# Third tile's slots written between the two half sums of the next tile, in the routing stage of a two-expert MoE layer

## The reference, cut to what matters

```python
y = mlstm_mixer(h, w_in, b_gates, head_norm_w, w_out)
h = layer_norm(ALPHA * h + y, ln1_g, ln1_b)
# hier_moe(h, ...):
g_top = argmax(h @ w_group + b_group)
within = (h @ w_router + b_router)[the 8 experts of g_top]
top_vals, top_idx = top_k(within, 2)
expert_ids = g_top * 8 + top_idx
# tokens are sorted by expert; each expert works on its own rows
yb = (silu(xb @ w_gate[e]) * (xb @ w_up[e])) @ w_down[e]
h = layer_norm(ALPHA * h + sum of the two weighted yb, ln2_g, ln2_b)
```

## Time and profile before

| | us |
|---|---|
| median of 3 runs | 1147.18 |
| lowest, highest | 1144.99, 1147.30 |
| the profiled execution, its own time | 1145.99 |
| its span in the trace | 1144.1 |
| PE busy | 1117.4 (98%) |
| DVE busy | 788.3 (69%) |
| ACT busy | 625.6 (55%) |

### The profile page before, as it was taken

One profiled execution on the slowest core, in us unless ns is written; L12 is line 12 of the kernel. 1 busy time (PEld: TensorE's weight loads), 2 busy tenths in 40 slices (PEclk: granted clock), 3 DMA queues, 4 the chain that ended last, 5 costly groups with the idle time before them and its releaser, 6 DMA issues.

```text
span 1144.1 us, 15458 instructions
## 1 busy us (share of the span) xinstructions
PE 1117.4 (98%) x5465; PEld 915.0 (80%) x5465; DVE 788.3 (69%) x1104; ACT 625.6 (55%) x692; POOL 209.4 (18%) x183
## 2 busy tenths in 40 slices
PE   8999999999999999999999999999999999999986
PEld 7878889778888787878888888888888888888852
DVE  3310323135455787779999999998988989899646
ACT  4311313213334410037888878788788887888634
POOL 3000111100000000002425312142332332322200
PEclk9999999999999998999999999999999999999998
DMA  7613314401211421138999999999999999999765
GB/s 279 208 50 120 120 45 129 129 19 39 72 39 57 184 93 56 74 152 340 417 389 366 399 378 383 398 383 392 380 374 384 380 391 384 381 397 379 284 272 222
DMA packets 65145, 284.23 MB, mean 248 GB/s; under 512 B 16156, under 2 KB 16156, under 8 KB 39620
## 3 DMA queue, kind: packets, MB, share of 16 engines
q1 hardware_dynamic: 52096, 254.14, 58.2%
q0 software_dynamic: 11840, 25.19, 6.0%
q10 hardware_dynamic: 1156, 4.20, 0.9%
HBM read 266.66 MB, written 33.55 MB: 262 GB/s over the span
## 4 chain that ended last, share of the span: by engine, by line
PE 92%; DVE 3%; DMA 2%; ACT 1%; issue 1%; DVEq 1%; POOL 0%; POOLq 0%; SPq 0%; ACTq 0%
PE bank L1582 26%; PE bank L1584 25%; PE bank L1583 25%; PE bank L1957 2%; PE bank L1846 1%; PE bank L1992 1%; PE bank L1797 1%; PE bank L1799 1%; PE bank L1802 1%; PE bank L1596 1%; PE bank L1755 1%; PE bank L1811 1%; DMA yy<-expert_rows 1%; PE bank L2055 1%; PE bank L1838 1%
## 5 line engine op out<-in xcount | busy, mean ns | idle before, releaser
L1582 PE MATMUL bank<-whi,xghi 128*128 128x512 f32 x512 | 202.5, 396 | 1.0 <-DVE xglo L1436 1.0
L1584 PE MATMUL bank<-whi,xglo 128*128 128x512 f32 x512 | 199.9, 390 | 0.0
L1583 PE MATMUL bank<-wlo,xghi 128*128 128x512 f32 x512 | 199.3, 389 | 0.0
L1424 DVE TENSOR_TENSOR wlo<-raw_down,whi 128x2048 fp32r<-128x2048 f32 x64 | 146.3, 2291 | 27.4 <-ACT whi L792 27.3
L1582 PE MATMUL bank<-whi,xhi 128*128 128x512 f32 x384 | 157.7, 411 | 1.1 <-ACT num L735 0.6
L1583 PE MATMUL bank<-wlo,xhi 128*128 128x512 f32 x384 | 152.6, 397 | 0.0
L1584 PE MATMUL bank<-whi,xlo 128*128 128x512 f32 x384 | 152.2, 396 | 0.0
L1424 DVE TENSOR_TENSOR wlo<-raw,whi 128x2048 fp32r<-128x2048 f32 x64 | 146.3, 2288 | 4.3 <-ACT whi L792 3.4
L1424 DVE TENSOR_TENSOR wlo<-raw_up,whi 128x2048 fp32r<-128x2048 f32 x64 | 146.3, 2285 | 0.0
L792 ACT ACTIVATE whi<-raw_up 128x2048 fp32r<-128x2048 f32 x64 | 122.4, 1914 | 25.8 <-PE bank L1584 25.4
L792 ACT ACTIVATE whi<-raw_down 128x2048 fp32r<-128x2048 f32 x64 | 122.4, 1912 | 23.1 <-PE bank L1584 23.1
(11 more groups left out here) (341 smaller groups left out, 1734.0 us busy)
## 6 DMA issues: line engine op xcount, KB each, us to landing
raw<-l_w_gate SPq DMA_DIRECT2D x64, 1024.0 KB, 8.2
raw_up<-l_w_up SPq DMA_DIRECT2D x64, 1024.0 KB, 8.4
raw_down<-l_w_down SPq DMA_DIRECT2D x64, 1024.0 KB, 8.6
raw<-l_w_in SPq DMA_DIRECT2D x5, 2048.0 KB, 10.2
yy<-expert_rows SPq DMA_DIRECT2D x7, 1024.0 KB, 13.1
xt<-hcat SPq DMA_DIRECT2D x8, 512.0 KB, 4.5
o_rows<-stage POOLq DMA_DIRECT2D x16, 256.0 KB, 2.4
qkT<-qk_rows SPq DMA_DIRECT2D x16, 256.0 KB, 3.9
```

Source lines behind the costliest of these rows:

```text
L1424: tt(wlo[k][:, halves(p)], raw_e[k][:, halves(p)], whi[k][:, halves(p)].bitcast(F32), ALU.subtract).then_inc(e_lo[k], 1)
L1582: t.matmul(out, lh, rh, start=first, stop=False)
L1583: t.matmul(out, lh, rl, start=False, stop=False)
L1584: return t.matmul(out, ll, rh, start=False, stop=last)
```

## The change

`norm_sums(3)` is replaced by its four parts, and `slots(2)` is put between the first and the second of them. No operation is added or taken away, apart from one drain (an instruction that waits until DVE's earlier operations have finished), which `slots` already had in front of it and `half_sums` has too. PE, ACT, POOL and SP have the program of before.

```diff
         residual(3, 0)
         residual(3, 1)
         top_two(2)
-        norm_sums(3)
+        half_sums(3, 0)
         slots(2)
+        half_sums(3, 1)
+        row_sums(3)
+        centre(3)
         norm_rows(3)
```

## The result

| | before | changed |
|---|---|---|
| median, us | 1145.82 (16 runs) | 1149.18 (16 runs) |
| lowest, highest | 1144.75, 1148.71 | 1147.67, 1150.21 |
| span of the profiled execution | 1144.1 | 1147.6 |

The ratio is 1.0022, with a 95% interval of 1.0015 to 1.0028: the change makes the kernel slower by 1.7 to 3.2 us, at the centre 2.5 us. The medians lie 3.36 us apart and the means of the runs 2.76: the times of each kernel fall into groups over a microsecond apart, so the centre depends on how it is taken. The forecast was 1148.3, with +1.1 us; the loss has its sign and is over twice as large. The kernel before was run again beside each set of experiments, with medians of 1147.73 (17 runs), 1147.48 (15) and 1147.31 (31), up to 1.9 us above the 1145.82 here. The changed kernel was not, apart from a single run, so part of the 2.5 us may belong to this set of runs.

The account below looks back on a forecast made before the run. PE, busy for 98% of the span, was taken to bound the kernel. -0.97 us won plus 2.05 us lost at half clock gave +1.08 on the median 1147.18: 1148.26, forecast as 1148.3, range 1145.3 to 1150.2.

Parts of the forecast that it names:

- `slots(2)` ahead lets `token_list(2)` start without a wait: On PE after out_half(4, 0): the wait for r_ohr goes, 2.31 us, with 0.11 us to spare.
- DVE pays nothing: On DVE from 443.40 to 447.31: reordering costs nothing, within 0.16 us either way; norm_rows(3) starts at 447.3 as before.
- PE runs ahead to `ranks(3)` and stands there: PE wins 5.59 us up to ranks(3), then waits 4.62 us for r_a; 0.97 us are left.
- A slow stretch behind `ranks(3)`: PE's dense products behind the wait run at half clock for 4.1 us, costing 2.05 us; bounds 1.7 and 3.4.
- the lower bound of +0.7: Low end of the net loss, +0.7 to +1.4 us, from slow stretches of 3.4 to 4.7 us.
- the low end of the forecast's own range, 1146.1: Own range 1146.1 to 1149.2: net +0.7 to +1.4 on runs 2.2 below to 0.1 above the median.
- The sum of +1.08 us: Whole kernel: -0.97 us won at ranks(3) plus 2.05 us lost at half clock, a loss of 1.08 us.
- It stays to the end: From out_half(4, 1) on: the +1.08 us persists, as PE's wait before ranks(4), 0.23 us at most, absorbs nothing.
- the rival of the later fall: Around 521 us the clock falls, slowing the first expert's products for 3.3 us: +1.65 more, 1149.9 us; chance 0.04.
- The long slow stretch: Rival: the slow stretch behind ranks(3) lasts 6.8 us, +2.4 us, 1149.6 us; chance 0.18.
- the clock hold: Rival behind ranks(3): PE's clock holds; chance 0.10.
- The gain as it looks: Rival at ranks(3): r_a isn't late, or PE keeps its 5.59 us: 1141.6 us; chance 0.06.

Follow-up runs that it names:

- Experiments 3: 18 fillers ahead of ranks(3) in the changed kernel: 1.0013 to before; 9 ahead of token_list(2) and 18 ahead of ranks(3) in the kernel before: 1.0040.
- 6: Changed kernel with inverse(3) and top_two(3) directly behind row_sums(3), and centre(3), shift(3) and residual(4, 0) behind them; ratio to before 0.9972.
- experiment 5: 4 + 4 fillers before and behind the transposes of the first expert's rows, in both kernels; ratios to before 0.9997 (kernel before) and 1.0007 (changed).
- experiment 7: Kernel before with only shift(3) and residual(4, 0) moved behind top_two(3), slots(2) still behind centre(3); ratio to before 0.9983.
- before, again: The kernel before, unchanged, run for a second trace; span 1147.6 us.
- 7, fillers of 5: Kernel before with shift(3) and residual(4, 0) behind top_two(3), plus 4 + 4 fillers at the first expert; ratio to before 0.9994.
- changed, again: The changed kernel, unchanged, run for a second trace; span 1148.1 us.
- 6, fillers of 5: Changed kernel with the choice of tile 3 ahead of centre(3), shift(3) and residual(4, 0), plus 4 + 4 fillers at the first expert; ratio to before 0.9970.
- experiment 1: Changed kernel with 38 filler matmuls on PE ahead of ranks(3); ratio to before 1.0043.

## Why the prediction was right, and where it wasn't

- *`slots(2)` ahead lets `token_list(2)` start without a wait.* Right. DVE had `r_ohr` ready at 446.14, PE came at 446.31.
- *DVE pays nothing.* Right: 3.94 us against 3.91 to `norm_rows(3)`.
- *PE runs ahead to `ranks(3)` and stands there.* Right: predicted 4.62 us from start to start, in the trace 455.58 less 451.09 (the last matmul's 450.86 and 0.23), 4.49; `ranks(3)` 0.97 us earlier, measured 0.98 and 0.99. Experiments 3 and 6 show that `r_a` is the cause.
- *A slow stretch behind `ranks(3)`.* Right in kind and too large in size: I took 4.1 us at half clock, 2.05 us lost. It was 3.4 us, and the stage lost 1.54, so its net is +0.56 in both pairs of traces without fillers (+0.48 in the pair of 5), just under the lower bound of +0.7. Half of the stretch was the wrong share, too: its matmuls come 0.43 us apart, and those at full clock 0.23, which is more than half of that, so 3.4 us lose 3.4 x (1 - 0.23 / 0.43) = 1.6 us and not 1.7. The prediction had 0.24 and 0.43 in its own rows and halved all the same.
- *Two slips in the working.* One half sum takes 0.69 us, as the rows of after show, but that isn't half of 1.46, since the row of two holds the gap between them; the gap of 0.08 us stands. And the low end of the forecast's own range, 1146.1, doesn't follow from its terms: 1147.18 - 2.2 + 0.7 is 1145.7.
- *The sum of +1.08 us as what the runs show.* This is the step that failed, though the sign is right; the measured centre is +2.5. It was made from one execution of before, in which the clock had fallen behind `slots(2)`'s wait for 6.8 us. That fall isn't certain: behind the same wait of 2.1 us the clock held in one trace of experiment 7 and fell in its sister. Where it holds in before, `ranks(3)` is there as early as in the changed kernel and nothing is slow behind it, and the stage's difference is 1.5 us instead of 0.56. Behind the wait of 4.3 to 4.4 us it fell in all three traces of the changed order. No trace of the kernel before itself shows a held clock (three of three fell, with that of 5), so this part of the account is inferred from the kernels of 7, whose PE does the same up to `ranks(3)`. The clocks of single runs point the same way: 12 of the 63 runs of before beside the experiments have a mean granted clock of 0.994 or 0.995, and times of 1144.6 to 1145.9 us. The first trace of before has 0.991, from 20.3 us at half clock (3.4 + 6.8 + 3.4, and 6.7 at the end, from 1137.4 on). By the same sum 0.994 is an estimate of 13.7 us, 6.6 less, about the length of that fall. This is likely, not shown.
- *"It stays to the end."* The shift did, tile by tile: (4) to (7) is 40.96 to 40.98 us in all four traces. But the rival of the later fall, which I gave 0.04, was there: at 524.2 us in both traces of the changed kernel and in one of two of before, 1.8 to 2.3 us each time. Taking it out of both kernels left 1.15 us of 2.5. It was mis-sized as a rare case on top of the change, while it is a common one for both kernels. Among the ten traces without fillers there, those of all variants, it comes in all five with the early `slots(2)` and in three of five with the late one. The times of the runs say more: all 16 of the changed kernel lie at 1147.67 us or above, in two groups (up to 1148.27, from 1149.12), and with the fillers of 5 such groups lie about 2 us lower (1145.49 to 1146.20, 1147.24 to 1148.30), as much as the fall costs, while the lowest run of before stays (1144.60 and 1144.69). So it seems to come in nearly every run of the changed kernel and not in every run of before. Why is not settled. The first of the two gaps, PE's wait for the gather, doesn't settle it: it was 0.71 us in the trace of before without the fall and 1.06 to 3.08 in the eight with it, but 1.25 in the trace of experiment 7 without fillers, where the clock held too.
- *The long slow stretch* behind `ranks(3)` (rival, 0.18) did not appear in three traces. Nor did the clock hold in these (it had 0.10 of the chances): it read 0.50 for 3.4 us behind `ranks(3)` in each. *The gain as it looks* is out.

The time, 1149.18, lies in the range, and that is luck in part. The range was laid around the median of three runs, 1147.18, and 16 runs put that median at 1145.82. From there the forecast would have been 1146.9 and the top of the range 1148.8, under what was measured. The chance of 0.23 for slower by over 0.2% was, for a ratio of 1.0022, too small.

## What to carry to other kernels

When a wait is taken from an in-order engine that another in-order engine feeds, work out when the feeder delivers the next item; if the feeder has no idle time up to there, the wait moves and only the difference is won (here 0.98 us of 5.6). Then move what the next item needs ahead of what it doesn't: the choice needed mean and deviation, not the normed row, and the two together gave 3 us, where the change alone lost and the early choice alone gave 0.7 to 2.0. And don't price a fall of TensorE's clock from one trace: take a second one (behind the same wait of 2.1 us it fell in four traces of five), and read the distances between fixed steps instead of the spans.

## What the runs showed of the hardware

The traces in which PE waited for over a microsecond around `ranks(3)`. The wait is the one that the timeline notes before `token_list(2)` or `ranks(3)`; the stretch at clock 0.50 is read to about 0.1 us.

| trace | PE's wait, us | for | clock at 0.50, us | length |
|---|---|---|---|---|
| before | 2.16 | `r_ohr` | 447.9 to 454.8 | 6.8 |
| before, again | 2.13 | `r_ohr` | 448.9 to 455.8 | 6.8 |
| before, fillers of 5 | 2.13 | `r_ohr` | 448.5 to 455.4 | 6.8 |
| 7, fillers of 5 | 2.13 | `r_ohr` | 448.7 to 455.6 | 6.8 |
| 7 | 2.14 | `r_ohr` | none, 1.00 from 440 to 500 | 0 |
| changed | 4.34 | `r_a` | 455.8 to 459.3 | 3.4 |
| changed, again | 4.34 | `r_a` | 455.9 to 459.4 | 3.4 |
| changed, fillers of 5 | 4.37 | `r_a` | 455.1 to 458.6 | 3.4 |
| 6 | 1.47 | `r_a` | none, 1.00 from 440 to 500 | 0 |
| 6, fillers of 5 | 1.46 | `r_a` | none, 1.00 from 440 to 500 | 0 |

- Behind the wait of 2.13 to 2.16 us, with the small matmuls of the list and the logits following it, the clock fell in four of these traces, for 6.8 us each, and held in one. Behind 4.34 to 4.37 us it fell in all three, for 3.4 us each. Behind 1.46 and 1.47 us it held in both.
- In the changed kernel's first trace the granted clock stays at 1.00 while PE stands still (451.3 to 455.5 us) and reads 0.50 only from 455.9 us on, when the work is back. In that of the changed kernel of experiment 5 it reads 0.50 from 455.2 us on, 0.3 us before the work is back at 455.51, and there `ranks(3)` to `ranks(4)` lost 0.18 us less (15.75 against 15.93).
- The stretch of 3.4 us at half clock on 512-column matmuls cost 1.53 us in the changed kernel, by `ranks(3)` to `ranks(4)` (15.93 us, against 14.40 with 18 fillers and no fall), and 1.6 by the sum from their distances, somewhat under half: they come 0.43 us apart in it (456.02 to 456.45) and 0.23 to 0.24 at full clock (459.60 to 459.84).
- The kernel before was at half clock near 230 us for 3.4 us in its first trace (232.9 to 236.4) and for 6.8 in its second (230.5 to 237.4), with `ranks(2)` at 442.91 and 444.23. From `ranks(7)` to the end it took 633.33 and 635.52 us, the second with the fall at 524 us on the first expert. The 31 runs of before beside the last experiments lie between 1144.6 and 1149.7 us.
- A fp32 filler of 128 columns took 0.223 us at clock 1.00 (38 of them from 451.18 to 459.66 in experiment 1), with two in the count for each (x76).
